# Input rows of a gated mixer block loaded already turned, their row factors spread by TensorE and multiplied in by VectorE

## The reference

```python
def _rmsnorm(x, g):
    y = xf * lax.rsqrt(jnp.mean(xf * xf, axis=-1, keepdims=True) + EPS)
    return (y * g.astype(jnp.float32)).astype(x.dtype)

h = _rmsnorm(x, norm_mix_g[layer])
proj = h @ w_in[layer]
gates = jax.nn.sigmoid((h @ w_gate[layer] + b_gate[layer]))
mkv = _rmsnorm(mem, norm_mem_g[layer]) @ w_mem_kv[layer]
```

## Time and profile before

| | us |
|---|---|
| median of three runs | 2591.25 |
| lowest and highest | 2591.13, 2591.43 |
| the profiled execution, as timed | 2593.32 |
| its span in the profile | 2591.5 |
| TensorE busy in it | 2565.0 (99%) |
| VectorE, ScalarE, GpSimd busy | 1734.6, 1157.6, 551.3 |

### The profile page before, as it was taken

How to read it: one execution, slowest core, us unless ns; L and a number is a source line. 1 busy time by engine, 2 the same in 40 slices (tenths; PEclk the granted TensorE clock), 3 DMA queues, 4 the chain that set the end, 5 groups by cost and what they waited for, 6 DMA issues and landing times.

```text
span 2591.5 us, 33051 instructions
## 1 busy us (share of the span) xinstructions
PE 2565.0 (99%) x12065; PEld 2128.1 (82%) x12065; DVE 1734.6 (67%) x2401; ACT 1157.6 (45%) x2131; POOL 551.3 (21%) x510
## 2 busy tenths in 40 slices
PE   8999999999999999999999999999999999999998
PEld 7888888888887887888887888888888888888887
DVE  7778657666466655658778666765557566575886
ACT  6344535344344433434456455654555243342533
POOL 1455200000022152336554333000000112111100
PEclk9999999999999999999999999999999999999999
DMA  4778555666446787787797666633355585767753
GB/s 146 253 241 258 199 183 179 186 216 225 144 136 240 236 258 256 230 276 260 231 298 230 229 220 197 218 110 118 110 172 162 114 221 109 185 150 161 201 179 114
DMA packets 346764, 508.71 MB, mean 196 GB/s; under 512 B 33208, under 2 KB 213484, under 8 KB 346604
## 3 DMA queue, kind: packets, MB, share of 16 engines
q1 hardware_dynamic: 318956, 431.08, 51.5%
q0 software_dynamic: 27648, 75.51, 11.8%
HBM read 325.12 MB, written 181.40 MB: 195 GB/s over the span
## 4 chain that ended last, share of the span: by engine, by line
PE 93%; DVE 4%; issue 1%; ACT 1%; DMA 1%; POOL 0%; SPq 0%; POOLq 0%; DVEq 0%
PE ps L2416 29%; PE ps L2418 29%; PE ps L2417 29%; PE ps L2421 2%; PE ps L2693 1%; PE ps L2670 1%; PE ps L2438 1%; DVE res_lo L1653 1%; DVE s_lo L1647 1%; PE ps L2593 1%; PE ps L2621 1%; DMA res_raw<-in_w_down 0%; DMA proj_d<-c 0%; ACT scores L1123 0%; DVE res_lo L1641 0%
## 5 line engine op out<-in xcount | busy, mean ns | idle before, releaser
L2416 PE MATMUL ps<-res_hi,s_hi 128*128 128x512 f32 x3084 | 1204.3, 391 | 6.4 <-issue 1.7
L2418 PE MATMUL ps<-res_hi,s_lo 128*128 128x512 f32 x3084 | 1200.9, 389 | 0.0
L2417 PE MATMUL ps<-res_lo,s_hi 128*128 128x512 f32 x3084 | 1200.9, 389 | 0.0
L2416 PEld LDWEIGHTS ps<-res_hi,s_hi 128*128 128x128 f32 x3084 | 579.1, 188 | 130.0 <-issue 6.1
L2418 PEld LDWEIGHTS ps<-res_hi,s_lo 128*128 128x128 f32 x3084 | 579.0, 188 | 120.7
L2417 PEld LDWEIGHTS ps<-res_lo,s_hi 128*128 128x128 f32 x3084 | 579.2, 188 | 118.1
L1123 ACT ACTIVATE s_hi<-piece_f 128x512 fp32r<-128x512 f32 x436 | 274.3, 631 | 478.6 <-PE ps L2418 420.6
L1123 ACT ACTIVATE s_hi<-s_sum 128x512 fp32r<-128x512 f32 x327 | 204.1, 628 | 367.5 <-PE ps L2418 338.6
L1647 DVE TENSOR_TENSOR s_lo<-piece_f,s_hi 128x512 fp32r<-128x512 f32 x432 | 322.6, 747 | 34.5 <-ACT s_hi L1123 26.5
L1647 DVE TENSOR_TENSOR s_lo<-s_sum,s_hi 128x512 fp32r<-128x512 f32 x327 | 247.8, 758 | 87.9 <-ACT s_hi L1123 87.7
L1707 DVE TENSOR_TENSOR u<-u,ps 128x512 f32<-128x512 f32 x109 | 74.8, 686 | 294.5 <-PE ps L2418 294.4
(11 more groups left out here) (195 smaller groups left out, 2501.7 us busy)
## 6 DMA issues: line engine op xcount, KB each, us to landing
proj_d<-c SPq DMA_DIRECT2D x152, 256.0 KB, 3.3
piece_f<-in_w_up SPq DMA_DIRECT2D x32, 1024.0 KB, 6.8
up_d<-c SPq DMA_DIRECT2D x128, 256.0 KB, 3.3
piece_f<-up_d SPq DMA_DIRECT2D x32, 1024.0 KB, 7.0
piece_f<-in_w_gate SPq DMA_DIRECT2D x24, 1024.0 KB, 7.1
w_hi<-parts_d SPq DMA_DIRECT2D x48, 512.0 KB, 3.7
w_lo<-parts_d SPq DMA_DIRECT2D x48, 512.0 KB, 5.2
temp<-proj_d SPq DMA_DIRECT2D x48, 512.0 KB, 6.8
```

The source lines that it names most:

```text
L2416: mm(dst, wh, xh, start=first, stop=False, skip_group_check=joins)
L2417: mm(dst, wh, xl, start=False, stop=False, skip_group_check=joins)
L2418: return mm(dst, wl, xh, start=False, stop=last, skip_group_check=joins)
```

## The change

A second copy of the rows of the five hosts is handed in already turned (`x_turned`, `mem_turned`), laid out so that one DMA of 1 MB with 8 KB in a row on each partition fills `ht` for a host. `load_rows` stays, for the sums of squares. In place of `norm_tiles`, ScalarE multiplies `ht` by the gain per column (`turned_weighted`, eight instructions of 128x2x128). GpSimd makes two diagonal matrices of the row factors (`diag_r`) right behind the power. TensorE multiplies a matrix of ones by such a diagonal, one fp32 matmul of 128x128 for each r, so that each partition of PSUM holds all 128 factors. VectorE multiplies `ht` by them in place (`turned_scaled`, two instructions of 128x512 for each r). Five semaphores go (their counts are joined to others), two come: xt_ld and dg_rdy. The hosts in the output projection stay as they were. Cut to its core, with the new functions whole:

```diff
+    ones = sb("ones", [P, 1])
+    diag_r = there("diag_r", [P, 2, P], 126)
@@ sync
+            def load_turned(n):
+
+                if n not in NORM_AT:
+                    return
+                if across(n):
+                    sp.wait_ge(hs_st, 64 * summed(n))
+                    for r in range(2):
+                        sp.wait_ge(ht_st[r], 16 * across(n))
+                else:
+                    sp.wait_ge(r_lo_done, PROD)
+                frm = a["mem_turned"] if n == MEM_AT else a["x_turned"][NORM_AT.index(n)]
+                sp.dma_start(ht[:], frm).then_inc(xt_ld, 16)
@@ sync, jobs
                             load_piece(n + 2)
+                    load_turned(n)
@@ scalar
+            def turned_weighted(n):
+
+                act.wait_ge(xt_ld, 16 * (across(n) + 1))
+                g0 = PM_MEM if n == MEM_AT else PM_MIX
+                for k in range(KT):
+                    last = op(ht[:, :, k, :], ht[:, :, k, :], ACT.Copy, scale=par[:, g0 + k:g0 + k + 1])
+                last.then_inc(xn_done, 2)
             def norm_tiles(n):
-                if not hosts(n):
+                if n in NORM_AT:
+                    turned_weighted(n)
+                if not out_job(n):
                     return
@@ vector
+            def turned_scaled(n, r):
+
+                dve.wait_ge(xt_rdy, 2 * across(n) + r + 1)
+                dve.wait_ge(xn_done, 2 * across(n) + 2)
+                by_row = ps[:, 6 + r, 0:P].rearrange("p (o n) -> p o n", o=1).broadcast_to([P, 4, P])
+                for h in range(2):
+                    half_row = ht[:, r, 4 * h:4 * h + 4, :]
+                    last = v.tensor_tensor(half_row, half_row, by_row, ALU.mult)
+                last.then_inc(ht_done, 1)
@@ gpsimd
             g_.memset(m_half[:], -0.5)
+            g_.memset(ones[:], 1.0)
@@ gpsimd, row_rms
                 g_.tensor_tensor(rrs[:], rvar[:], m_half[:, 0:2], ALU.pow).then_inc(rs_pow, 1)
+                if n in NORM_AT:
+                    pool.wait_ge(rs_pow, normed(n) + 1)
+                    if across(n):
+                        pool.wait_ge(xt_rdy, 2 * across(n))
+                    else:
+                        pool.wait_ge(r_lo_done, PROD)
+                    for r in range(2):
+                        g_.tensor_scalar(diag_r[:, r, :], ident[:], rrs[:, r:r + 1], None, ALU.mult).then_inc(dg_rdy, 1)
@@ tensor
+            def factors_across(n, r):
+
+                pe.wait_ge(dg_rdy, 2 * across(n) + r + 1)
+                if 2 * across(n) + r:
+                    pe.wait_ge(ht_done, 2 * across(n) + r)
+                mm(ps[:, 6 + r, 0:P], ones[:].broadcast_to([P, P]), diag_r[:, r, :], start=True, stop=True).then_inc(xt_rdy, 1)
             def rows_across(n, r):
-                if not hosts(n):
+                if n in NORM_AT:
+                    factors_across(n, r)
+                if not out_job(n):
                     return
```

More of the change, by code:

```diff
@@ L394, in build @@
     setup = sem("setup")
-    ident_rdy = sem("ident_rdy")
     par_rdy = sem("par_rdy")
@@ L403, in build @@
     pad_rdy = sem("pad_rdy")
-    upad_rdy = sem("upad_rdy")
     w_ld = [sem(f"w_ld{i}") for i in range(WS)]
@@ L439, in build @@
     pooled_lo = sem("pooled_lo")
-    wp_tr = sem("wp_tr")
     b_ld = [sem("b_ld0"), sem("b_ld1")]
@@ L488, in build @@
     with_gain = sem("with_gain")
-    gf_ld = sem("gf_ld")
+    xt_ld = sem("xt_ld")
+    dg_rdy = sem("dg_rdy")
     def kp(w):
@@ L898, in jobs @@
                         sp.dma_start(g_fin[:], a["norm_final_g"].rearrange("(o n) -> o n", o=1).broadcast_to([P, D]))\
-                            .then_inc(gf_ld, 16)
+                            .then_inc(late_ld, 16)
                     if n + 1 >= LAST_DOWN and adds_rows(n + 1):
@@ L1276, in pool_rows_high @@
             def pool_rows_high():
-                act.wait_ge(wp_tr, 1)
+                act.wait_ge(misc_done, 2)
                 for g in range(GROUPS):
@@ L1552, in chained @@
                 dve.wait_ge(d, steps[0])
-            dve.wait_ge(setup, 1)
+            dve.wait_ge(setup, 2)
             chained(v.tensor_scalar(dist[CHUNK:P, :], dist[CHUNK:P, :], -float(CHUNK), None, ALU.add))
@@ L1800, in take_ht @@
                         dve.wait_ge(hs_st, 64 * summed(n))
-                g0 = PM_MLP if out_job(n) else PM_MEM if n == MEM_AT else PM_MIX
                 for h in range(2):
                     last = v.tensor_tensor(ht[:, r, 4 * h:4 * h + 4, :],
-                                           ps[:, 6 + h, :].rearrange("p (k n) -> p k n", n=P), gain(g0, h), ALU.mult)
+                                           ps[:, 6 + h, :].rearrange("p (k n) -> p k n", n=P), gain(PM_MLP, h), ALU.mult)
                 last.then_inc(ht_done, 1)
@@ L1880, in jobs @@
                     if n == LAST_DOWN + 1:
-                        dve.wait_ge(gf_ld, 16)
+                        dve.wait_ge(late_ld, 48)
                         chained(v.tensor_scalar(g_fin[:], g_fin[:], float(D) ** 0.5, None, ALU.mult))
@@ L2199, in _ @@
             g_ = nc.gpsimd
-            g_.memset(ident[:], 0.0).then_inc(ident_rdy, 1)
+            g_.memset(ident[:], 0.0).then_inc(setup, 1)
             g_.memset(m_half[:], -0.5)
+            g_.memset(ones[:], 1.0)
             g_.iota(dist[:], [[-1, WIN_KEYS]], base=CHUNK, channel_multiplier=1,
@@ L2204, in _ @@
             g_.iota(pos[:], [[1, PAD]], base=1, channel_multiplier=0, allow_small_or_imprecise_dtypes=True)
-            pool.wait_ge(ident_rdy, 1)
+            pool.wait_ge(setup, 1)
             g_.affine_select(out=ident[:], in_=ident[:], compare_op=ALU.not_equal, fill=1.0, base=0,
                              pattern=[[-1, P]], channel_multiplier=1).then_inc(setup, 1)
-            pool.wait_ge(setup, 1)
+            pool.wait_ge(setup, 2)
             def row_scales(p):
@@ L2368, in jobs @@
                         pool.wait_ge(mk_kept, 16 * (VISITS // 2))
-                        g_.memset(u_pads[0][:, :, 0:PAD], 0.0).then_inc(upad_rdy, 1)
-                        pool.wait_ge(upad_rdy, 1)
+                        g_.memset(u_pads[0][:, :, 0:PAD], 0.0).then_inc(pad_rdy, 1)
+                        pool.wait_ge(pad_rdy, 1)
                         windows(0)
@@ L2421, in transpose @@
                 return nc.tensor.transpose(dst, src, ident[0:n, 0:n])
-            pe.wait_ge(setup, 1)
+            pe.wait_ge(setup, 2)
             pe.wait_ge(row_ld, 96)
@@ L2554, in pool_rows_across @@
                     last = transpose(ps[:, 6, g * P:(g + 1) * P], wp_st[:, g, :])
-                last.then_inc(wp_tr, 1)
+                last.then_inc(misc_done, 1)
             def fuse_pool(u):
@@ L2751, in mixers @@
             def mixers():
-                pe.wait_ge(pad_rdy, 1)
+                pe.wait_ge(pad_rdy, 2)
                 pe.wait_ge(ev_dve, POSTS * (IN_END - 1) + U3)
@@ L2805 @@
         aps[name] = nc.dram_tensor(f"in_{name}", arrays[f"in_{name}"].shape, F32, kind="ExternalInput").ap()
+    x, mem = inputs["x"][0], inputs["mem"][0]
+    turned = {"x_turned": x[SEQ // 2:].reshape(2, 4, P, KT, P).transpose(1, 4, 0, 3, 2),
+              "mem_turned": mem.reshape(2, P, KT, P).transpose(3, 0, 2, 1)}
+    for name, laid in turned.items():
+        arrays[f"in_{name}"] = np.ascontiguousarray(laid)
+        aps[name] = nc.dram_tensor(f"in_{name}", arrays[f"in_{name}"].shape, F32, kind="ExternalInput").ap()
     out = nc.dram_tensor("out", (1, SEQ, D), F32, kind="ExternalOutput").ap()
```

1 line of the change is left out of this document (added).

## The result

The changed kernel takes 2597.34 us (median of 8 runs, 2595.81 to 2604.90), the kernel before took 2591.43 (8 runs beside it, 2591.13 to 2591.93). The ratio is 1.0026, 95% interval 1.0017 to 1.0035: **5.9 us slower**, where 2.9 us faster was forecast. The profiled execution was the slowest of the eight, 2604.90 with a span of 2602.7. So its waits are probably larger than those of a median run, and it is read here for where the time went; a second profile of the same kernel (run e10) shows by how much this varies.

What follows compares the result with a forecast made beforehand. TensorE was taken to bound the kernel: 5.8 us saved on the transposes, less a 2.9 us stall at host 10 behind GpSimd, gives -2.9, from 2591.25 to 2588.4 us; range 2585.3 to 2592.8.

Steps and rivals of the forecast that it cites:

- What bounds the kernel: TensorE, busy 2565.0 of 2591.5 us: work it drops comes off the time if nothing it waits for is late.
- TensorE, fp32 matmuls in: Ten fp32 matmuls replacing the hosts' transposes on TensorE: 0.21 us each, 2.1 in all (1.0 to 3.2); saved 5.8.
- ScalarE, VectorE, the head, SP: ScalarE's weightings, VectorE's scaling, GpSimd's setup memset: nothing on the path; SP with its added loads is not late.
- The price of a load: Each added 1 MB on SP delays GpSimd's weight store by 1.9 us, bounds nothing to 3.7.
- The Trainium skill's rule: DMA engines alternate between queues by packet; in piece 10 the store's delay would be under 1 us; not used.
- I count the pair at nothing for the next host: GpSimd's two diagonals per host, 1.20 us at the head, cost the next host nothing; the following load waits for stores anyway.
- The burst of piece 9 lies between them: GpSimd's delay from piece 7 does not add to piece 10's: the later store waits less than 8.07 us in piece 9.
- delays add up: Rival: piece 7's delay persists on GpSimd into piece 10, stall 4.8 to 8.4 us, time 2590.3 to 2593.9; chance 0.22.
- Host 7 "just in time": At host 7 the diagonal is ready at 201.9 us, TensorE comes at 202.6, so no stall.
- No term for TensorE's clock: The prediction counted a TensorE stall by GpSimd as lost once, 2.9 us at host 10, with nothing for a lower clock.
- slower: Rival: GpSimd's weight loop with three loads at 3.7 and two pairs at 1.2 unhidden, stall 14.5, time 2600; chance 0.04.

Runs made afterwards that it cites:

- e10: The changed kernel run once more with no edit, on one chip with the repeats e11 and e12; 2598.77 us, ratio 1.0027.
- e1: The changed kernel with GpSimd's weight sums moved to pieces where they are not ahead of a host's factors; 2585.86 us, ratio 0.9980.
- e3: The changed kernel with the 1 MB load whole only at host 1, 64 bytes per partition at hosts 4, 7, 10, 13; 2585.46 us, ratio 0.9982.
- e11: e1 run once more with no edit, on the same chip as e10 and e12; 2585.96 us, ratio 0.9981.
- e6: The changed kernel with 1 MB loads whole only at hosts 1 and 10, 64 bytes per partition at the others; 2588.99 us, ratio 1.000.
- e9: The changed kernel with 1 MB loads whole only at hosts 1 and 7, 64 bytes per partition at the others; 2589.93 us, ratio 0.9992.
- e7: The changed kernel with 1 MB loads whole only at hosts 1, 4 and 7, 64 bytes per partition at the others; 2594.38 us, ratio 1.0013.
- e2: The kernel before with only the five 1 MB loads added, their data overwritten by VectorE; 2593.74 us, ratio 1.0012.
- e12: e4 run once more with no edit, on the same chip as e10 and e11; 2593.98 us, ratio 1.0010.
- e4: The changed kernel with each host's two diagonals made by ScalarE instead of GpSimd; 2594.14 us, ratio 1.0012.
- e8: The kernel before with only the weight sums' table changed as in e1; 2591.36 us, ratio 1.0002.
- e5: e1 with TensorE's r = 0 matmul at each host held back by chains of small VectorE operations; 2626.36 us, ratio 1.0141.

## Why the prediction was wrong

In short, three steps failed: GpSimd's delay was to end at the burst of piece 9, and 5.8 to 7.3 us of it came through; a load was priced at 1.9 us, and the passes of pieces 7 and 10 grew by 3.9 to 7.4; and no term stood for TensorE's clock, which took 3.2 to 4.6 (each from e10 and the profile of after). The terms one by one:

**What bounds the kernel: right.** What TensorE no longer does comes off the time where nothing is late: e1, e3 and e11 show 5.3 to 5.7 us.

**TensorE, fp32 matmuls in: the term was mis-sized, in the change's favour.** 0.14 us each instead of 0.21, which is inside the bounds. The estimate came from eight in a row; one that stands between fp32r matmuls costs less. The saving is 6.5, not 5.8. The return of 0.32 was as assumed.

**ScalarE, VectorE, the head, SP: right.** The eight weightings take 3.30 us for a host, 1.1 more than the two instructions did, and TensorE waited for neither ScalarE nor VectorE there.

**The price of a load: mis-sized.** 1.9 was taken from the pair, with bounds of 0 and 3.7. A load makes its pass 2 to 5 us longer by itself (e6, e9, piece 4 of e7), 1.7 to 6.9 in e2, and in the changed kernel the passes of pieces 7 and 10 are 25.4 and 25.5 us, 6.8 and 6.3 more than before. Two things were wrong in the reading. The pair of rows doesn't differ by exactly one load: in piece 9 the store is issued 2.6 us behind SP's last load, in piece 10 5.0 behind, and 256 KB of `ht` are stored beside the first. And in piece 7 the piece's load wasn't nearer its end than in piece 10. It was issued at 173.81, 4.9 us ahead of the store; the waits of 4.35 and 6.20 so differ by 1.9 with no load added at all, as much as the price that was taken.

Besides, a pass also has the next load of `tin` in it. In pieces 7 and 10 of the ten profiles with the weight sums in pieces 2 to 11, the way from that load to the next store takes 13.7 to 15.6 us where SP's load of the next piece is issued within 1.1 us of it (191.90 and 191.42 in the rows of after above), and 11.0 to 13.1 where that comes 1.5 us or more behind. This too is read from times, and no run changed it alone.

The Trainium skill's rule, on the page "DMA: Bandwidth & Descriptors", section "Queues, rings and completion order", is that an engine goes round between its queues by packets. From it the prediction derived less than 1 us. No run here bears that size out: the smallest price of any pass is 1.7 us (e2, piece 10), the others are about 2 and more. What failed may be the derivation and not the rule: it took the SP queue as filled anyway.

**"I count the pair at nothing for the next host": failed.** It was true of the 1.2 us themselves, which the wait for the stores swallows. It overlooked that the weight store behind them is moved too, from ahead of SP's load of the rows to behind it, where it waits 11.4 us. With the loads present the pair costs 4.8 us (e12 against e10), and without it host 7 doesn't stall.

**"The burst of piece 9 lies between them": the step that turned the sign.** The delay of piece 7 was to end there. The effect that it counted on is real: a store issued later waits less beside SP's burst. The burst of piece 9 took up 2.4 of 4.3 us in e9, 1.2 of 8.5 in the profile of after and 2.7 of 8.5 in e10; that of piece 6 took up 7.1 of 9.4 in after. But 7.3 us (after) and 5.8 (e10) were left at the store of piece 9, against before, where the prediction had nothing. Either is above the 4.8 us that it gave itself as the point where the change turns into a loss. The prediction named this under "delays add up", gave it 0.22, and held the very observation that speaks for it, no idle time ahead of either host's factors.

**Host 7 "just in time": failed.** Its factors come 9.2 us later than before, where 1.9 was forecast and 3.7 the bound, and TensorE waits 6.3 us. Of the 9.2, 2.3 are what the burst of piece 6 has left of the delays of piece 2 and of host 4's load, and 6.8 come in the pass of piece 7 itself (in e10 1.6 and 7.4).

**No term for TensorE's clock: the step that was missing.** 4.6 us in the profile of after, 3.2 in e10. All rivals took a wait as lost once. It was lost once and more than a third over again.

The rival that happened is *slower*, whose mechanism was the weight loop with three loads and two pairs not hidden. It gave 2600 for 0.04; the median was 2597.34. Of its parts, 11.1 for the loads and 2.4 for the pairs sum to 13.5 at host 10, and the factors there came 13.6 later than before (273.47 and 259.87). That the sum fits so well is luck: neither part is of the size that it gives, there was a stall at host 7 as well, and in e10, nearer the median run, the factors come 9.7 later. In after, 7.3 of the 13.6 were there at the store of piece 9, 2.7 more come from the wait for that store and 3.6 from the rest of the pass.

What stays open: why the pass of piece 7 takes 25 to 26 us in e7, after and e10, and 21 to 22 in e4, e9 and e12, with the same load beside it, for which the nearness of the two loads named above is a candidate; why a pass without a load scatters by 2.6 us in piece 10; and what sets the length of the slow stretch. Also why e1 and e11 gain 5.3 us where ten groups at 0.65 make 6.5: at the point behind the last host e1 is 6.3 us ahead of e8 (465.5 and 471.8), so the saving is there, and up to 1 us is lost again behind it. And why eight runs of the changed kernel spread over 9 us, where 31 of the kernel before spread over 3.2. Its two profiles differ by 3.8 us of wait at host 10, so a loop without slack that depends on the order of transfers is the likely cause, but this was only argued.

The version that beats both is e1: 2585.9 and 2586.0 in its two comparisons, 5.3 us faster than before, and 12.8 faster than the changed kernel on the same chip.

## What to carry to other kernels

When work is moved off the bounding engine, look at the engine whose result it now waits for, and at what that engine's queue holds ahead of it. If there is no idle time but DMA waits, an added transfer is paid there, and its delay reaches the next result in part: the waits beside another queue's burst shrank and took up 1 to 7 us of it here, but in the changed kernel not all. What such a transfer costs isn't one number either, 1.7 to 7.7 us here, by what it happens to meet. Such a queue is cured by moving the background task, not by making the foreground faster: here one table of ten numbers was worth 12.8 us. And a wait of TensorE of 2 us or more should be priced above its length, in this kernel by 1.5 to 3 us.

## What the runs showed of the hardware

- Behind waits of 1.9 to 11.75 us TensorE's granted clock read 0.50, for 4 to 14 matmuls of 128x512 that started 0.43 us apart instead of 0.23 (in e2 for the eight transposes ahead of them too), 1.5 to 3 us in all. Behind waits of 0.94 (e5) and 1.19 us (e2) it stayed at 1.00. In e6 the first two matmuls of 128x512 behind the wait still went at full pace, in e9 the first four. TensorE of e6 at host 10:

```profile
261.09 0.49 PE L2521 MATMUL ps<-diag_r,ones 128*128 128x128 f32 x2 [1.90 <-POOL diag_r L2300]
261.33 0.48 PE L2463 MATMUL ps<-res_hi,s_hi 128*128 128x512 f32 x1
261.64 0.40 PE L2464 MATMUL ps<-res_lo,s_hi 128*128 128x512 f32 x1
261.88 0.60 PE L2465 MATMUL ps<-res_hi,s_lo 128*128 128x512 f32 x1
262.27 0.63 PE L2463 MATMUL ps<-res_hi,s_hi 128*128 128x512 f32 x1
```

- One fp32 matmul of 128x128 between fp32r ones costs 0.14 us, little more than one fp32 transpose of that size (0.10).
- A load of 1 MB more on SP's queue made a pass of stores, loads and sums on GpSimd's queue 1.7 to 7.7 us longer (17.8 to 20.4 us without it, 20.9 to 26.0 with it). A delay of that chain shrank by 1 to 7 us where its store met a burst of two loads on SP's queue: in after the wait was 3.51 us instead of 10.56 in piece 6.
- GpSimd waited 5.8 and 6.3 us for the same 1 MB store when it was issued 1.6 us ahead of another queue's load (e5, e12), and 11.4 when issued 0.1 us behind it (e1, after).
